# Two query chunks of layer 1 computed from the un-normalised residual, and the adaLN weights placed behind the query weights in the ring

## The chip, the cores and the metric

The kernel runs on one core of one Trainium2 chip. The metric is the device time of one execution in microseconds (us), the median of several runs. A core has five engines that run side by side and meet at semaphores: PE (TensorE, matrix products into the PSUM banks), ACT (ScalarE), DVE (VectorE), POOL (GpSimd) and SP (SyncE, which here only issues DMA transfers from HBM). All tiles live in SBUF, 128 partitions wide.

## The reference, cut to what matters

Two post-norm layers over 512 latent and 256 context tokens, width 1024. Layer 0 ends with a SwiGLU FFN and a layer norm; layer 1 begins with adaLN modulation of that result and one input projection:

```python
x = _layer_norm(ALPHA * x + ml[5] * _swiglu(_modulate(x, ml[3], ml[4]), ...), ln_g[l, 1], ln_b[l, 1])   # end of layer 0
# layer 1
ml = jnp.split(sc @ mod_w[l] + mod_b[l], 6, axis=-1)          # adaLN: six vectors of 1024, also for ctx
h_lat = x * (1.0 + ml[1]) + ml[0]
qk, v, og, g = jnp.split(h @ w_in, [o1, o2, o3], axis=-1)      # w_in: 1024 x (512 q + 512 k + 1024 v + 1024 og + 32 gates)
qk = jax.nn.silu(_centred_conv(qk, conv_w, conv_b))            # 3 taps over the tokens
g = (g.reshape(b, s, 4, H_M) + gate_b)                         # input and forget gates, then log_sigmoid and scans
```

Queries are needed for the latent tokens alone. With r the residual before the layer norm, x is (r - mean) * rstd * ln_g + ln_b, so a product with x can be made as a product with r and mended by mean and rstd of each token afterwards.

## The kernel before

Every product is made in three passes: weights and inputs are split into a high part (fp32r) and the rest, and PE forms high*high, high*low and low*high (`project`, line 692). Activations lie transposed: 8 chunks k of 128 features by 768 tokens (`xT`).

**The ring.** SP streams all weights through `ring`, 4 slots of 128x1024 fp32 (512 KB, a "unit"), in the fixed order of `STAGES`. `slot_free` makes SP wait until the unit four places ahead was used up. A projection unit is used up when POOL has made its low part (ACT copies the high part in `split_high`, POOL subtracts in `split_low`, line 2369, and counts `lo_made`). An adaLN unit (`mod` stages) is used by PE as it is, fp32, in `mod_rows_stacked` (line 644, 4 products of 256 columns, shown by the profile as 8 matmuls), which counts `unit_done`.

**Around the change.** The last third of the FFN of layer 0 writes its 8 output tiles m; after each, DVE updates `xT` (`z_update`), ACT squares it, DVE and POOL add up sum and sum of squares. Then PE does, in this order: adaLN units 0 to 2 of vector 2, the two cross-partition sums of the layer norm (`ln_sums`, line 964), the other 5 units of vector 2 and the 8 of vector 3. Beside it the layer norm runs through DVE and ACT, and chunk by chunk ACT makes the modulated input of layer 1 (`next_input`, lines 1294 and 1297) and DVE its low part (`low_chunk`, line 1767). ACT splits the first two projection units after its chunks 6 and 7. PE then starts the q/k chunks f = 0 and 1 (f = 0 to 3 are queries, 24 matmuls of 512 columns; 4 to 7 keys, 48 matmuls of 512 or 256) and the gate product on the padded tile `wg`, interleaved; then f = 2 to 7, and `token_major` (line 680) for the values.

**Gates and convolution.** ACT evacuates the gates (lines 1599), DVE and ACT form log-sigmoid (lines 2156, 1628, 1629, 2174), and DVE runs eight scans (line 2180, a cumulative sum and a running maximum, two directions, two token ranges). In between it does the 3-tap convolution of chunk f (`conv(f)`, lines 2169 to 2171) on what `conv_in(f)` of ACT put into `cpad`. `mod_columns` (PE transposes at line 652, DVE copy at line 1756, which counts `mod_ev`) turns a finished adaLN row into columns. The order on every engine is written out by hand.

## Time and profile before

| what | us |
|---|---|
| median of 3 runs | 1905.59 |
| lowest, highest | 1902.66, 1906.91 |
| the profiled execution, its own time | 1901.86 |
| span of its trace | 1900.1 |
| PE busy | 1776.1 (93%) |
| DVE, ACT, POOL busy | 688.1, 607.5, 716.1 |
| granted PE clock, mean | 0.97 |

The trace counts from the first instruction of the span. PE is busy for 93% of it, and the row of 40 slices shows one clear hole in it outside the first slice and the mLSTM: slice 25 (about 1140 to 1188 us), where its digit is 6, the granted clock falls to 0.7, and the DMA digit rises to 6. That is the stretch that the change touches.

### The profile page before, as it was taken

What the parts mean: (1) busy time and instruction counts of PE and PEld (TensorE: products, weight loads), DVE (VectorE), ACT (ScalarE), POOL (GpSimd) and SP (SyncE); (2) the same over time, 40 slices, a digit from 0 to 9 for tenths busy, and PEclk for the clock granted to TensorE, in tenths of its full rate; (3) what the DMA queues carried; (4) which work ended last, traced back from release to release, by engine and by line L of the source; (5) the groups of instructions that cost most, each with busy time, mean ns of one, the idle gap of its engine ahead of it and who ended that gap; (6) DMA issues with size and microseconds to landing.
All of it is one profiled execution on the core that took longest, in us unless ns stands there. A gap on an engine that the chain in (4) does not pass through costs nothing.

```text
span 1900.1 us, 24466 instructions
## 1 busy us (share of the span) xinstructions
PE 1776.1 (93%) x9848; PEld 1424.3 (75%) x9848; DVE 688.1 (36%) x1187; ACT 607.5 (32%) x863; POOL 716.1 (38%) x378
## 2 busy tenths in 40 slices
PE   4999999899899999999999996999776989999998
PEld 2788767455588888888888883787565878888886
DVE  2134254566467511111111036750178761111114
...
GB/s 295 121 47 62 58 122 89 103 165 177 111 56 65 58 67 78 56 67 57 76 58 53 50 61 207 56 69 66 55 1 23 89 70 108 111 89 100 88 83 72
DMA packets 210986, 163.36 MB, mean 86 GB/s; under 512 B 17742, under 2 KB 191022, under 8 KB 210902
## 3 DMA queue, kind: packets, MB, share of 16 engines
...
q14 instruction: 26, 0.21, 0.0%
...
## 4 chain that ended last, share of the span: by engine, by line
PE 82%; DVE 10%; ACT 4%; issue 2%; DMA 2%; POOL 1%; ACTq 0%; POOLq 0%; DVEq 0%
PE ps L692 58%; PE ps L680 3%; PE ps L682 3%; PE ps L681 3%; PE ps L851 2%; PE ps L878 2%; PE ps L903 1%; PE ps L888 1%; PE ps L805 1%; DMA ring<-in_mod_w 1%; PE ps L634 1%; PE ps L644 1%; DVE xT L2002 1%; PE ps L789 1%; DVE xT L1992 1%
## 5 line engine op out<-in xcount | busy, mean ns | idle before, releaser
L2375 POOL TENSOR_TENSOR wsplit<-ring,wsplit 128x1024 fp32r<-128x1024 f32 (+1 forms) x136 | 326.0, 2411 | 521.2 <-ACT wsplit L1470 521.0
L692 PE MATMUL ps<-hhi,wsplit 128*128 128x512 f32 (+1 forms) x1920 | 473.1, 354 | 6.4 <-DVE hu L2041 6.4
L692 PEld LDWEIGHTS ps<-hhi,wsplit 128*128 128x128 f32 x1920 | 314.9, 188 | 60.0 <-DVE hu L2041 6.9
L692 PE MATMUL ps<-hlo,wsplit 128*128 128x512 f32 x960 | 288.0, 354 | 0.0
L692 PE MATMUL ps<-uhi,wsplit 128*128 128x512 f32 x1008 | 250.4, 353 | 0.0
L2118 DVE TENSOR_TENSOR hu<-sg,ps 128x768 f32<-128x768 f32 (+1 forms) x40 | 32.9, 821 | 438.1 <-ACT sg L1539 438.1
L1470 ACT ACTIVATE wsplit<-ring 128x1024 fp32r<-128x1024 f32 (+1 forms) x136 | 135.1, 1023 | 173.5 <-PE ps L692 173.5
L692 PEld LDWEIGHTS ps<-uhi,wsplit 128*128 128x128 f32 x1008 | 164.9, 188 | 27.6
L692 PEld LDWEIGHTS ps<-hlo,wsplit 128*128 128x128 f32 x960 | 157.5, 188 | 26.5
L1965 DVE SCALAR_TENSOR_TENSOR xT<-ps,modc,xT 128x512 f32<-128x512 f32 x96 | 60.6, 659 | 272.1 <-PE ps L692 250.4
L692 PE MATMUL ps<-ulo,wsplit 128*128 128x512 f32 x504 | 150.8, 353 | 0.0
L2433 POOL TENSOR_SCALAR lnbuf<-lnbuf,den 128x768 f32<-128x768 f32 (+1 forms) x48 | 85.1, 1778 | 173.1 <-DVE den L1923 172.5
L1539 ACT ACTIVATE sg<-ps 128x768 f32<-128x768 f32 (+1 forms) x40 | 28.3, 706 | 377.2 <-PE ps L692 377.2
L692 PE MATMUL ps<-hx,wsp_in 128*128 128x256 f32 (+3 forms) x672 | 125.2, 347 | 6.5 <-POOL wsp_in L2369 6.5
L692 PEld LDWEIGHTS ps<-hx,wsp_in 128*128 128x128 f32 (+1 forms) x672 | 104.2, 189 | 26.8 <-POOL wsp_in L2369 6.9
L2369 POOL TENSOR_TENSOR wsp_in<-ring,wsp_in 128x1024 fp32r<-128x1024 f32 x22 | 53.2, 2416 | 168.3 <-ACT wsp_in L1285 168.3
L2369 POOL TENSOR_TENSOR wlo<-ring,whi 128x1024 fp32r<-128x1024 f32 x24 | 59.4, 2473 | 127.8 <-ACT whi L1285 127.8
L692 PEld LDWEIGHTS ps<-ulo,wsplit 128*128 128x128 f32 x504 | 82.5, 188 | 13.9
L692 PE MATMUL ps<-hx,wsp_out 128*128 128x512 f32 (+1 forms) x384 | 68.1, 340 | 2.5 <-DVE hx L2056 2.5
L692 PEld LDWEIGHTS ps<-hx,wsp_out 128*128 128x128 f32 x384 | 58.9, 188 | 11.7 <-DVE hx L2056 2.7
L2369 POOL TENSOR_TENSOR wsp_out<-ring,wsp_out 128x1024 fp32r<-128x1024 f32 x16 | 41.4, 2590 | 62.6 <-ACT wsp_out L1285 62.6
L680 PE MATMUL ps<-whi,hT 128*128 128x512 f32 x160 | 63.8, 399 | 0.8 <-ACT mv L1658 0.8
...
## 6 DMA issues: line engine op xcount, KB each, us to landing
...
```

The source lines that it names most:

```text
L680: pe.matmul(dst, s_hi, m_hi, start=first, stop=False)
L681: pe.matmul(dst, s_hi, m_lo, start=False, stop=False)
L682: return pe.matmul(dst, s_lo, m_hi, start=False, stop=last)
L692: mm = pe.matmul(dst[:, a:b], w, h[:, a:b], start=st, stop=sp_)
L851: mm = pe.matmul(pair[:, a:b], w, cqkv[:, k0 + k, a:b], start=(k == 0), stop=(k == nk - 1))
L878: mm = pe.matmul(PS[it % 2][:, a:b], qs_[0:DQ, q, tq], ks_[0:DQ, k, a:b], start=st, stop=sp_)
L1470: act.activation(w_part(s, 0)[:, 0:width], ring[:, (NB[f"ffn{l}"] + s) % RING, 0:width], ACT.Copy).then_inc(hi_made, 1)
L1965: ins = dve.scalar_tensor_tensor(xT[:, m, a:b], pair[:, a:b], modc[:, l, g, m, v:v + 1], xT[:, m, a:b], ALU.mult, ALU.add)
L2118: dve.tensor_tensor(hu[:, jj, 0:nt], sg[:, jj, 0:nt], PS[2 * jj][:, 0:nt], ALU.mult).then_inc(h_done, 1)
L2369: pool.tensor_tensor(w_lo[:, i % 2, :], ring[:, n % RING, :], w_hi[:, i % 2, :].bitcast(F32), ALU.subtract).then_inc(lo_made, 1)
L2375: pool.tensor_tensor(w_part(s, 1)[:, 0:width], ring[:, (NB[f"ffn{l}"] + s) % RING, 0:width], w_part(s, 0)[:, 0:width].bitcast(F32), ALU.su ...
L2433: pool.tensor_scalar(probs(i)[:, a:T], probs(i)[:, a:T], den[:, 1, i:i + 1], None, ALU.mult).then_inc(att_p, 1)
```

## The change

Chunks f = 0 and 1 are now made from the residual. While the last FFN tiles run, ACT makes `zqhi` = the high part of `xT` times the gain of layer 1 (`gain[:, 1, 0]`), DVE its rest `zqlo`, and two extra columns (minus the gain, and the shift) are put beside the 512 tokens, so that their products give what the mean and the shift have to be multiplied by. The weights of f = 0 and 1 pass the ring behind the FFN units and are split like those into `wsplit`. After the FFN, PE does f = 0 (48 matmuls of 256 or 258 columns), `ln_sums`, and f = 1; `late_query` on DVE mends them with mean and rstd, and ACT adds the shift in `conv_in`.

The adaLN units go elsewhere: units 0 to 2 of vector 2 are loaded into a tile of their own, `mod_pre`; units 3 and 4 and the weights of f = 2 and 3 share the ring; units 5 to 7 of vector 2 and all 8 of vector 3 come behind them. PE does f = 2 and 3 along with the arriving input chunks, then these 11 adaLN units, then the gate product, and then f = 4 to 7. ACT splits the two weight units after its input chunks 0 and 1. `mod_columns` of vector 3 is now called at f = 5 and done by DVE behind `conv(3)`, and its end is waited for at f = 6.

The core of the diff:

```diff
+    QW = LAT + 2
+    zqhi, zqlo, mod_pre = under(("zqhi", [P, KD, QW], F32R), ("zqlo", [P, KD, QW], F32R), ("mod_pre", [P, 3, UNIT], F32))
...
+    N_Q = 2
...
-              ("mod11", KD), ("mod05", KD), ("mod14", KD), ("mod15", KD), ("out0", N_OUT), ("ffn0", N_FFN), ("mod12", KD), ("mod13", KD), ("in1", N_IN1),
+              ("mod11", KD), ("mod05", KD), ("mod14", KD), ("mod15", KD), ("out0", N_OUT), ("ffn0", N_FFN + N_Q), ("mod12", 2), ("in1", 2), ("mod12b", 3), ("mod13", KD), ("in1b", N_IN1 - 4),
...
+    def q_bank(f):
+        return PS[(2, 3, 0, 1, 2, 0, 1, 2)[f]]
...
-        mod_units(1, 2)
-        mod_units(1, 3)
+        sp.wait_ge(ffn_tile, FT[0] + N_FFN - KD + TILE_CREDIT)
+        for k in range(MOD_PRE):
+            sp.dma_start(mod_pre[:, k, :], mod_w[1, k * P:(k + 1) * P, 2 * D:3 * D]).then_inc(mod_pre_in, 16)
         w_in = m_w_in[0].rearrange("(k p) n -> p k n", p=P)
-        for i in range(N_IN1):
-            n = NB["in1"] + i
+        for i in range(N_Q):
+            n = NB["ffn0"] + N_FFN + i
+            slot_free(n)
+            unit(n, view(n % RING, KD), w_in[:, :, i * P:(i + 1) * P])
+        mod_units(1, 2, MOD_PRE, MOD_PRE + 2)
+        for i in range(N_Q, N_IN1):
+            if i == 4:
+                mod_units(1, 2, MOD_PRE + 2, KD, "b")
+                mod_units(1, 3)
...
+        pe.wait_ge(zq_cols, 1)
         pe.wait_ge(z_ev, ZB[1] - 1)
-        mod_rows_stacked(1, 2, half(4), 0, 3)
-        ln_sums(1)
-        mod_rows_stacked(1, 2, half(4), 3, KD)
-        mod_rows_stacked(1, 3, half(5))
+        for f in range(N_Q):
+            pe.wait_ge(lo_made, FB[0] + N_FFN + f + 1)
+            if f == 1:
+                pe.wait_ge(z_ev, ZB[1])
+            for k in range(KD):
+                if f == 0:
+                    pe.wait_ge(zq_lo, k + 1)
+                for w, z, st, sp_ in ((0, zqhi, k == 0, False), (0, zqlo, False, False), (1, zqhi, False, k == KD - 1)):
+                    for a, b, at in LATE_MM[1]:
+                        mm = pe.matmul(q_bank(f)[:, at:at + b - a], w_part(f, w)[:, k * P:(k + 1) * P], z[:, k, a:b], start=st, stop=sp_)
+            mm.then_inc(ffn_tile, 1)
+            if f == 0:
+                ln_sums(1)
+        rows2, rows3 = PS[0][:, T:], PS[1][:, T:]
+        pe.wait_ge(ln_mean, 2)
+        pe.wait_ge(ln_var, 2)
+        pe.wait_ge(mod_pre_in, 16 * MOD_PRE)
+        for k in range(MOD_PRE):
+            for b in range(4):
+                pe.matmul(rows2[32 * b:32 * b + 2, :], s_kv[:, k, :], mod_pre[:, k, 256 * b:256 * (b + 1)], start=(k == 0), stop=False)
+        mod_rows_stacked(1, 2, rows2, MOD_PRE, MOD_PRE + 2)
...
-        for k in range(KD + 2 * LAG):
+        for k in range(KD + LAG):
             if k < KD:
                 pe.wait_ge(input_lo, 2 * KD + k + 1)
-            for f, kf in ((0, k), (1, k - LAG)):
+            for f, kf in ((2, k), (3, k - LAG)):
...
-            kf = k - 2 * LAG
-            if 0 <= kf < KD:
-                if kf == 0:
-                    pe.wait_ge(gate_lo, 1)
-                mm = project(PS[3], wg[:, 0, kf, :], wg[:, 1, kf, :], hT1[:, kf, :], hlo1[:, kf, :], kf == 0, kf == KD - 1, ALL_SEGS)
-                if kf == KD - 1:
-                    mm.then_inc(gate_mm, 1)
-        mod_columns(1, 2, half(4))
-        for f in range(2, 8):
-            if f == 2:
+        mod_rows_stacked(1, 2, rows2, MOD_PRE + 2, KD, "b")
+        mod_rows_stacked(1, 3, rows3)
+        pe.wait_ge(gate_lo, 1)
+        pe.wait_ge(late_q, 2)
+        for k in range(KD):
+            mm = project(PS[3], wg[:, 0, k, :], wg[:, 1, k, :], hT1[:, k, :], hlo1[:, k, :], k == 0, k == KD - 1, ALL_SEGS)
+        mm.then_inc(gate_mm, 1)
+        mod_columns(1, 2, rows2)
+        for f in range(4, 8):
+            if f == 5:
+                mod_columns(1, 3, rows3)
                 pe.wait_ge(mod_ev, MOD_AT[1, 2])
-            if f == 5:
+            if f == 6:
                 pe.wait_ge(mod_ev, MOD_AT[1, 3])
-            if f >= 3:
+            if f >= 5:
                 pe.wait_ge(f_ev, f - 2)
-            if f == 3:
-                mod_columns(1, 3, half(5))
             split_unit("in1", f)
             for k in range(KD):
                 mm = m_chunk(f, k)
             mm.then_inc(unit_done, 1)
         in1_parts = ((whi1, wlo1), hT1, hlo1)
-        token_major("in1", 8, [(t, t) for t in (4, 5, 0, 1, 2, 3)], *in1_parts, lambda b: pe.wait_ge(f_ev, (7, 8, 6)[b // 2]))
+        token_major("in1", 8, [(t, t) for t in range(TT)], *in1_parts, lambda b: pe.wait_ge(f_ev, (6, 7, 8)[b // 2]))
...
-            split_after = {0: (0, 1), 2: (6, 7)}.get(i)
+            split_after = (0, 1) if i in (0, 2) else None
...
+                if i == 2 and k == 0:
+                    act.wait_ge(ffn_tile, FT[0] + N_FFN + N_Q + TILE_CREDIT)
...
+                    if third == 2 and l == 0:
+                        if m == 0:
+                            act.wait_ge(gains_ok, 2)
+                        act.activation(zqhi[:, m, 0:LAT], xT[:, m, 0:LAT], ACT.Copy, scale=gain[:, 1, 0, m, 0:1]).then_inc(zq_hi, 1)
...
-        from_norm(1, hT1, hlo1_raw, lambda i: split_high("in1", i, whi1))
+        from_norm(1, hT1, hlo1_raw, lambda i: split_high("in1", i + N_Q, whi1))
...
-        split_high("in1", 2, whi1)
-        act.wait_ge(gate_mm, 1)
-        for g, dst in enumerate((li, gt, li, gt)):
-            act.activation(dst[0:H_M, g // 2, :], PS[3][32 * g:32 * g + H_M, 0:T], ACT.Identity,
-                           bias=gb[32 * g:32 * g + H_M, :]).then_inc(gate_ev, 1)
...
-            if f >= 2:
+            if f >= 4:
                 split_high("in1", f + 2, whi1)
-            act.wait_ge(unit_done, UB["in1"] + f + 1)
-            if f < 2:
+            if f < N_Q:
                 act.wait_ge(pad_ok, 4)
-            else:
-                act.wait_ge(conv_done, f - 1)
-            ins = act.activation(cpad[:, f % 2, 1:1 + LAT], PS[f % 3][:, 0:LAT], ACT.Copy)
+                act.wait_ge(late_q, f + 1)
+                act.activation(cpad[:, f, 1:1 + LAT], cacc[:, f, 0:LAT], ACT.Identity, bias=qc[:, f, 1:2]).then_inc(f_ev, 1)
+                return
+            act.wait_ge(unit_done, UB[part_of("in1", f)] + f + 1)
+            act.wait_ge(conv_done, f - 1)
+            ins = act.activation(cpad[:, f % 2, 1:1 + LAT], q_bank(f)[:, 0:LAT], ACT.Copy)
...
-        conv_in(0)
-        split_high("in1", 3, whi1)
+        for f in range(N_Q):
+            conv_in(f)
+            split_high("in1", f + 4, whi1)
+        act.wait_ge(gate_mm, 1)
+        for g, dst in enumerate((li, gt, li, gt)):
+            act.activation(dst[0:H_M, g // 2, :], PS[3][32 * g:32 * g + H_M, 0:T], ACT.Identity,
+                           bias=gb[32 * g:32 * g + H_M, :]).then_inc(gate_ev, 1)
...
+        def late_query(f):
+            dve.wait_ge(ffn_tile, FT[0] + N_FFN + f + 1 + TILE_CREDIT)
+            step(dve.tensor_copy(qc[:, f, :], q_bank(f)[:, LATE_COL[1]:LATE_COL[1] + 2]))
+            for a, b, at, _ in LATE_TOKENS[1]:
+                ins = dve.scalar_tensor_tensor(cacc[:, f, a:b], lnm[:, a:b], qc[:, f, 0:1], q_bank(f)[:, at:at + b - a], ALU.mult, ALU.add)
+            step(ins)
+            dve.tensor_tensor(cacc[:, f, 0:LAT], cacc[:, f, 0:LAT], lnr[:, 0:LAT], ALU.mult).then_inc(late_q, 1)
...
+                zq_low(KD - 1)
                 layer_norm(1, (hT1, hlo1, hlo1_raw))
...
-                mod_rows_stacked(1, 2, half(4))
-                mod_columns(1, 2, half(4))
-                mod_rows_stacked(1, 3, half(5))
+                for f in range(N_Q):
+                    late_query(f)
+                mod_rows_stacked(1, 2, PS[0][:, T:], "b")
...
         conv(0)
-        mod_columns(1, 3, half(5))
+        conv(1)
+        mod_columns(1, 2, PS[0][:, T:])
+        mod_rows_stacked(1, 3, PS[1][:, T:])
+        dve.wait_ge(gate_ev, 4)
+        dve.scalar_tensor_tensor(g_, z_, -1.0, z_, ALU.mult, ALU.min).then_inc(ls_in, 1)
+        dve.wait_ge(ls_ln, 1)
+        step(dve.scalar_tensor_tensor(b_, z_, 0.0, b_, ALU.min, ALU.subtract))
         for d in range(2):
             scan(gbc, lf, d, ALU.add, 0.0)
-        conv(1)
+        conv(2)
         step(dve.tensor_tensor(li[0:H_M, :, :], li[0:H_M, :, :], g_, ALU.subtract))
         for d in range(2):
             scan(gt, li, d, ALU.max, 0.0)
-        conv(2)
+        conv(3)
+        mod_columns(1, 3, PS[1][:, T:])
         dve.tensor_scalar(negm[0:H_M, :, :], gt[0:H_M, :, 0:LAT], -1.0, None, ALU.mult).then_inc(rows_ok, 1)
         dve.tensor_tensor(gbc[0:H_M, :, 0:LAT], gbc[0:H_M, :, 0:LAT], gt[0:H_M, :, 0:LAT], ALU.add).then_inc(floor_in, 1)
-        for f in range(3, 8):
+        for f in range(4, 8):
...
-        split_low("in1", 0, whi1, wlo1)
-        split_low("in1", 1, whi1, wlo1)
```

SP's DMA issues from the end of the FFN of layer 0 on, in the kernel before (`in_mod_w` are adaLN weights, `in_m_w_in` the projection weights of layer 1; a count is for issues alike):

```order
L496 DMA ring<-in_mod_w 128x1024 [waits lo_made] x4
L496 DMA ring<-in_mod_w 128x1024 [waits unit_done] x12
L496 DMA ring<-in_m_w_in 128x8x128 [waits unit_done] x4
L496 DMA ring<-in_m_w_in 128x8x128 [waits lo_made] x4
L496 DMA ring<-in_m_w_in 128x2x512 [waits lo_made] x8
```

The same place in the changed kernel:

```order
L607 DMA mod_pre<-in_mod_w 128x1024 [waits ffn_tile]
L607 DMA mod_pre<-in_mod_w 128x1024 x2
L517 DMA ring<-in_m_w_in 128x8x128 [waits lo_made] x2
L517 DMA ring<-in_mod_w 128x1024 [waits lo_made] x2
L517 DMA ring<-in_m_w_in 128x8x128 [waits lo_made] x2
L517 DMA ring<-in_mod_w 128x1024 [waits unit_done] x2
L517 DMA ring<-in_mod_w 128x1024 [waits lo_made] x2
L517 DMA ring<-in_mod_w 128x1024 [waits unit_done] x7
L517 DMA ring<-in_m_w_in 128x8x128 [waits unit_done] x4
```

The two first query units moved ahead of all adaLN units of the ring, two more stand between them, and a run of 7 adaLN units that each wait for PE (`unit_done`) stands ahead of the other projection weights.

PE between the last adaLN units and the input projection, before (lines 644 adaLN, 692 projection):

```order
L644 MATMUL ps<-ring,scol 2x256 x3
L644 MATMUL ps<-ring,scol 2x256 [waits landed0]
L644 MATMUL ps<-ring,scol 2x256 x3
L644 MATMUL ps<-ring,scol 2x256 [waits landed1]
L644 MATMUL ps<-ring,scol 2x256 x3
L692 MATMUL ps<-hT,whi 128x512 [waits input_lo,lo_made,z_ev,ln_rstd]
L692 MATMUL ps<-hlo,whi 128x512
L692 MATMUL ps<-hT,wlo 128x512
L692 MATMUL ps<-hT,whi 128x512 [waits input_lo]
```

The changed kernel, behind chunks f = 2 and 3 (lines 674 adaLN, 722 projection):

```order
L674 MATMUL ps<-ring,scol 2x256 x3
L674 MATMUL ps<-ring,scol 2x256 [waits landed1]
L674 MATMUL ps<-ring,scol 2x256 x3
L674 MATMUL ps<-ring,scol 2x256 [waits landed2]
L674 MATMUL ps<-ring,scol 2x256 x3
L722 MATMUL ps<-hT,wg 128x512 [waits late_q,gate_lo]
L722 MATMUL ps<-hT,wg 128x256
L722 MATMUL ps<-hlo,wg 128x512
L722 MATMUL ps<-hlo,wg 128x256
```

What follows the last adaLN unit is now the gate product, which was interleaved with f = 0 and 1.

DVE around the column copy of vector 3 (`modc`), before; `gbc` scans are cumulative sums, `cacc` rows are one convolution:

```order
L2174 SCALAR_TENSOR_TENSOR lf<-gt,lf 8x1536 [waits ls_ln]
L2169 TENSOR_SCALAR cacc<-cpad,vcol 128x512 [waits f_ev,dve_step]
L2170 SCALAR_TENSOR_TENSOR cacc<-cpad,vcol,cacc 128x512 [waits dve_step]
L2171 SCALAR_TENSOR_TENSOR cacc<-cpad,vcol,cacc 128x512 [waits dve_step]
L1756 TENSOR_TENSOR modc<-ps,modb 128x8 [waits mod_T]
L1756 TENSOR_TENSOR modc<-ps,modb 128x8
L2180 SCALAR_TENSOR_TENSOR gbc<-lf 8x256
L2180 SCALAR_TENSOR_TENSOR gbc<-lf,gbc 8x512 [waits dve_step]
```

The changed kernel; `gt` scans are the running maxima:

```order
L2254 SCALAR_TENSOR_TENSOR gt<-li 8x256 [waits dve_step]
L2254 SCALAR_TENSOR_TENSOR gt<-li,gt 8x512 [waits dve_step]
L2254 SCALAR_TENSOR_TENSOR gt<-li 8x256 [waits dve_step]
L2254 SCALAR_TENSOR_TENSOR gt<-li,gt 8x512 [waits dve_step]
L2246 TENSOR_SCALAR cacc<-cpad,vcol 128x512 [waits silu_ev,f_ev,dve_step]
L2247 SCALAR_TENSOR_TENSOR cacc<-cpad,vcol,cacc 128x512 [waits dve_step]
L2248 SCALAR_TENSOR_TENSOR cacc<-cpad,vcol,cacc 128x512 [waits dve_step]
L1809 TENSOR_TENSOR modc<-ps,modb 128x8 [waits mod_T]
L1809 TENSOR_TENSOR modc<-ps,modb 128x8
L2274 TENSOR_SCALAR lnbuf<-gt 8x1024
L2275 TENSOR_TENSOR gbc<-gbc,gt 8x2x512
```

The copy moved from behind the first convolution to behind all eight scans and the convolution of f = 3.

## Rows read from the trace of the kernel before

**Rows 1.** Chain that ended last, 1050 to 1260: start us, us, engine, tile, line.

```profile
1168.47 0.84 ACT hT L1297
1169.32 0.96 ACT whi L1285
1170.34 2.37 POOL wlo L2369
1172.84 21.60 PE ps L692 x96
...
1235.02 8.65 PE ps L692 x48
```

**Rows 2.** Stretches: length, busy PE PEld DVE ACT POOL, PEclk, DMA share, GB/s.

```profile
1150.00:1160.00 10.00, 3.72 (x32) 0.44 (x32) 10.00 (x11) 7.76 (x11) 2.93 (x2) 0.65 0.97 318
```

**Rows 3.** Timeline of PE, 1139 to 1180: start us, us, what, [idle before].

```profile
1141.73 1.48 PE L644 MATMUL ps<-ring,scol 128*2 128x256 f32 x24
...
1145.85 1.56 PE L964 MATMUL ps<-lnbuf,kc 128*128 128x512 f32 x4 [0.21 <-POOL lnbuf L2399]
...
1160.53 1.04 PE L644 MATMUL ps<-ring,scol 128*2 128x256 f32 x8 [1.72 <-DMA ring<-in_mod_w]
...
1165.72 1.03 PE L644 MATMUL ps<-ring,scol 128*2 128x256 f32 x8 [0.24 <-DMA ring<-in_mod_w]
1172.84 0.76 PE L692 MATMUL ps<-hT,whi 128*128 128x512 f32 x1 [6.09 <-POOL wlo L2369]
...
1177.09 0.39 PE L692 MATMUL ps<-hlo,whi 128*128 128x512 f32 x1
...
1179.86 0.40 PE L692 MATMUL ps<-hlo,whi 128*128 128x512 f32 x1
```

**Rows 4.** Stretch of layer 1 in products of 256 columns: length, PE busy, PEclk, DMA.

```profile
1525.00:1530.00 5.00, 5.00 (x44) 1.00 0.35 100
```

**Rows 5.** Timeline of ACT, 1095 to 1250.

```profile
1154.70 1.31 ACT L1294 ACTIVATE hlo_raw<-xT,gain 128x512 f32<-128x512 f32 x2 [2.15 <-DVE xT L2002]
...
1169.22 1.04 ACT L1285 ACTIVATE whi<-ring 128x1024 fp32r<-128x1024 f32 x1
...
1197.22 0.90 ACT L1599 ACTIVATE gt<-ps,gb 8x768 f32<-8x768 f32 x1
...
1202.73 1.58 ACT L1629 ACTIVATE lf<-lf,onec 8x1536 f32<-8x1536 f32 x1
```

**Rows 6.** Timeline of DVE, 1095 to 1270.

```profile
1172.37 1.15 DVE L1767 TENSOR_TENSOR hlo<-hlo_raw,hT 128x768 fp32r<-128x768 f32 x1 [2.06 <-ACT hT L1297]
...
1204.34 1.75 DVE L2174 SCALAR_TENSOR_TENSOR lf<-gt,lf 8x1536 f32<-8x1536 f32 x1 [4.44 <-ACT lf L1629]
1206.12 2.55 DVE L2169 TENSOR_SCALAR cacc<-cpad,vcol 128x512 f32<-128x512 f32 x1
...
1209.89 0.75 DVE L2171 SCALAR_TENSOR_TENSOR cacc<-cpad,vcol,cacc 128x512 f32<-128x512 f32 x1
...
1213.55 1.27 DVE L2180 TENSOR_TENSOR_SCAN gbc<-lf,gbc 8x512 f32<-8x512 f32 x1
...
1221.73 3.44 DVE L2180 TENSOR_TENSOR_SCAN gt<-li,gt 8x512 f32<-8x512 f32 x1
...
1227.62 0.49 DVE L2169 TENSOR_SCALAR cacc<-cpad,vcol 128x512 f32<-128x512 f32 x1
...
1228.93 0.75 DVE L2171 SCALAR_TENSOR_TENSOR cacc<-cpad,vcol,cacc 128x512 f32<-128x512 f32 x1
```

**Rows 7.** Timeline of POOL, 1085 to 1270.

```profile
1205.81 2.58 POOL L2369 TENSOR_TENSOR wlo<-ring,whi 128x1024 fp32r<-128x1024 f32 x1 [3.50 <-ACT whi L1285]
```

**Rows 8.** Tile ring, the issue by SP at 1142.4: an adaLN unit into an idle queue.

```profile
DMA to landing us min/median/max: 4.0/4.0/4.0
```

**Rows 9.** Groups by form, 1350 to 1800: count | busy us, mean ns | idle before.

```profile
L2016 DVE SCALAR_TENSOR_TENSOR zlo<-xT,gain,zhi 128x512 fp32r<-128x512 f32 x8 | 8.7, 1082 | 0.0
...
L1462 ACT ACTIVATE zhi<-xT,gain 128x512 fp32r<-128x512 f32 x8 | 5.7, 711 | 6.5 <-DVE xT L1965 6.5
```

86 lines of the change are left out of this document (53 added, 33 removed).

## The prediction

> **What bounds the kernel now.** I read the 40 slices first: PE is the engine that sets the time, with one hole at the layer boundary. The chain of waits of that stretch [rows 1] shows how the hole ends: ACT works through input chunks of 128 features, splits the first weight unit only behind its seventh chunk, POOL makes the low part (2.37 us), and PE starts the input projection at 1172.84. The timeline of PE [rows 3] shows it done with the FFN at 1141.7, so 31.1 us lie between, in which it did 16 adaLN units and the layer-norm sums. In that hole the granted clock was 0.65 and the DMA engines were busy for 0.97 [rows 2]: the adaLN units come as fast as HBM gives them, one per 1.3 us at the end ((1165.72 - 1160.53)/4, [rows 3]). From 1172.84 on PE is nearly gapless, and the last query/key chunk ends at 1235.02 + 8.65 = 1243.67 [rows 1], which is the mark that I carry the sum to. Everything behind it is the same work in the same order, so the difference at that mark is the difference of the kernel.
>
> **The change, step by step.** Times are those of the trace of before, so the sum is made against that execution.
>
> Tail of the FFN. Each output tile gets one more ACT pass and one more DVE pass; the alike operations of layer 1 take 711 and 1082 ns [rows 9]. ACT and DVE wait for PE there, so they cost nothing; if the last pair were late, PE would stand for at most their sum, 1.8 us, and its own 42 matmuls on the chunks before (4.8 us) cover that.
>
> A, the late query chunks. A layer-1 product of this shape runs 44 matmuls in 5.00 us [rows 4], so 48 take 5.45. f = 0 runs from 1141.7 to 1147.2, then come the two sums of 1.56 us each [rows 3], to 1150.3. Before they ended at 1145.85 + 1.56 = 1147.41. The layer norm starts 2.9 us later, and with it everything on ACT and DVE. f = 1 and the five first adaLN units run beside the layer norm, to about 1158.3.
>
> B, the input chunks. The first starts at 1154.70 + 2.9 = 1157.6 [rows 5]. Seven chunks took 1154.70 to 1169.31 [rows 5, 1], 2.09 each; eight, with two splits of 1.0 [rows 5] now among them, end at 1176.3, the last low part (1.15, [rows 6]) at 1177.5. PE follows chunk by chunk with f = 2 and 3, and has 12 matmuls left behind the last one. At full clock one takes 0.231 ((1179.86 - 1177.09)/12, [rows 3]), so they end at 1180.3. Here the change is well ahead: all four query chunks are done, while before f = 0 and 1 and the gate product ran until 1194.44 (1172.84 + 21.60, [rows 1]). At half clock PE would need (1177.09 - 1172.84)/10 = 0.425 for each of 48 from about 1163.4 on, and end at 1183.8; I take 1180.3, since dense work brought the clock back after 4 us in [rows 3].
>
> C, the adaLN stream. Four units are in the ring when PE gets to them, but the next slot comes free only when PE has used the first, at 1180.8. A transfer into an idle queue took 4.0 us [rows 8]: 1184.8. Six more follow. They come at 1.3 us at best; over the whole stream before, with 1.04 us of matmuls for each in the round, the pitch was up to 1.7, since other transfers stood between. I take 1.4, near the undisturbed end: 1193.2, and 1.0 us for the last unit's matmuls: 1194.2. That is 13.9 us in which PE works for some 6. Before, the same wait lay under the layer norm and was free. Bounds: 1193.1 and 1196.3.
>
> The Trainium skill ("DMA: Bandwidth & Descriptors", Specifications) gives a core about 358 GB/s from HBM. By that a unit of 524,288 bytes takes 1.46 us and the stream would end 0.4 us later than mine, an estimate from that page; the trace had one each 1.3.
>
> D, the gate product. It no longer shares PE's wait for input chunks; it starts behind the stream. It has the 48 matmuls of a key chunk: 8.65 us [rows 1]. After the hole before, the first ten matmuls took 4.25 instead of 2.31 [rows 3], so I add 1.9, PE having been idle for more than half of C: it ends at 1204.8. Before it ended at 1194.44. Lower bound without the 1.9.
>
> E, gates to log-sigmoid. The same operations: from 1194.44 to the end of the Ln at 1202.73 + 1.58 = 1204.31 [rows 5], 9.9 us: 1214.7. PE meanwhile does f = 4 (from 1205.5), waits for the evacuation of f = 2, which ACT now does behind the Ln (about 1215.3), and does f = 5, to 1224.0.
>
> F, the wait of f = 6. Its bank holds the row of vector 3 until DVE has copied the columns, and that copy stands behind everything on the gates. Before, DVE went from 1204.34 to 1228.93 + 0.75 = 1229.68, 25.3 us [rows 6], through the same eight scans with three convolutions; now there are two between, as two are done ahead of the gates. The one that goes took 1206.12 to 1210.64, 4.5 us, which leaves 20.8. In it one convolution and one scan were slow: a tensor_scalar of 2.55 where the same took 0.49, a scan of 3.44 where another took 1.27 [rows 6]. The slow tensor_scalar began 0.3 us behind the start of a POOL subtraction and ended 0.3 behind its end [rows 6, 7]. The weight splits of units 6 and 7 fall into this stretch; by my schedule unit 6 meets the convolution of f = 2 and unit 7 just misses the scan. So 20.8 - 2.2 = 18.6: the copy is made at 1233.3. Bounds: 16.2 with no meeting, 23.3 with every operation slow. PE stands from 1224.0 to 1233.3.
>
> G, f = 6 and 7. 8.65 each, and 1.9 again for the clock after 9 us of idling: 1252.5. Against 1243.67 that is +8.8.
>
> The copies, `mod_pre` and the waits that remain cost nothing: `mod_pre` is loaded while the FFN tail runs, `late_query` (two columns and three passes a chunk, done under C: at up to 1.1 us a pass [rows 9] some 6 of its 13.9 us), and the bank order of the values asks for each evacuation when it is due. Were that cover missing, the last evacuation would be late by about one convolution.
>
> **The sum.** 1901.86 + 8.8 = 1910.7 for an execution like the profiled one. The median of the runs is 3.7 above the profiled one, so I forecast 1905.6 + 8.8 = 1914.4, and write 1914. With all lower bounds (C -1.1, D -1.9, F -2.4, G -1.9) it is +1.5; with all upper ones (B +3.5, C +2.1, F +4.7) it is +19.1. The likeliest case's own range is 1909 to 1919.
>
> **The rivals.** Anything within 0.2% (3.8 us) is what a measurement here cannot tell from no change.
>
> *Faster, by a short wait at f = 6.* If DVE makes the column copy by the time f = 5 ends, F is not on the path: f = 6 and 7 follow at once, 1224.0 + 17.3 = 1241.3, 2.4 better than before; with C at its 1.3 pitch and no clock loss in D, E ends at 1211.7 and f = 7 at 1238.2, which is -5.4: 1900. For it: two whole query chunks leave the busy stretch, and convolutions 0 and 1 are made under C. Against it: it needs E's end to copy in about 9 us, and the eight scans and the two long passes over 1536 columns alone are more than that. It decides at a copy before about 1222.
>
> *No change to tell.* The lower bounds together: POOL misses DVE and the clock stays up. +1.5, so 1907. For it: [rows 6] shows each operation also at its short time. Against: the 6.09 us of idling before were followed by half clock [rows 3], and C and F are that long.
>
> *Slower still, by the shared port.* In F every POOL subtraction falls on DVE. Then F is 23.3 and the total +13.5: 1919. For it: in the gate stretch before, the convolution and the scan of [rows 6] were hit. The Trainium skill ("SBUF — State Buffer", Who interferes with whom) says that whichever of POOL and a DVE instruction of two SBUF inputs or of a two-port mode starts first keeps the other out until it has finished. By that rule the convolution's other passes block too. The trace agrees with the rule in the pair named in F; where the subtractions fall is not shown.
>
> **How the numbers follow.** Forecast 0.56, shared port 0.10, no change 0.20, faster 0.14. So slower by over 0.2%: 0.66, within: 0.20, faster: 0.14. The range of 1903 to 1920 leaves out most of the faster case and little above.
>
> **What would show it.** Right: the sums end near 1150, PE follows the input chunks from about 1163, a run of adaLN groups each idle for DMA from 1182 to 1194, the gate product ends at 1203 to 1206, and f = 6 has an idle time of some 9 us put down to the `modc` copy. Wrong, each by its own step: adaLN groups without idle before them (C), a half clock during f = 2 and 3 (B), or an f = 6 that follows f = 5 without a gap (F). The last alone turns the sign.

## The result and the profile after

The changed kernel takes 1917.44 us (median of 7 runs, 1914.02 to 1927.83) against 1905.59 of the kernel before in the same session. The ratio is 1.0077, with an interval of 1.0054 to 1.0100, so the change costs 14.7 us (10.3 to 19.1) of 1905.59. I had forecast slower by 8.8. The direction was right, the size too small. The profiled execution took 1917.19 us, its span 1915.5, at a granted clock of 0.963 (before 0.970).

The executions differ by up to 18 us before they reach the changed stage: the FFN of layer 0 ends at 1137 us in one of them and at 1156 in another. So every place below is counted from the end of that FFN's last matmul, at 1141.81 before and 1142.88 after (the expectations count from 0.17 us earlier in the changed kernel). By that count the tokens' product, which starts where f = 7 ends, moved from +101.7 to +114.6: 12.9 us. From there to the end of the span it takes 656.6 us before and 658.0 after.

These are PE's waits of the changed kernel from 1140 to 1290: tile and line, the releaser, us in total, times, longest.

```profile
PE ps L722 <- DVE modc L1809: 11.3, 1, 11.3
PE ps L722 <- POOL wlo L2450: 10.0, 1, 10.0
PE ps L674 <- DMA ring<-in_mod_w: 5.3, 7, 2.4
```

The first is the wait of f = 6 for the column copy, the second that of f = 2 for its weights' low part, the third the adaLN stream. Here is the stream on PE's timeline (start, us, what, idle before it), then the first step of f = 6.

```profile
1183.33 1.91 PE L674 MATMUL ps<-ring,scol 128*2 128x256 f32 x32
1187.65 0.61 PE L674 MATMUL ps<-ring,scol 128*2 128x256 f32 x8 [2.41 <-DMA ring<-in_mod_w]
...
1196.33 1.03 PE L674 MATMUL ps<-ring,scol 128*2 128x256 f32 x8 [0.66 <-DMA ring<-in_mod_w]
1197.29 1.01 PE L722 MATMUL ps<-hT,wg 128*128 128x512 f32 x2
...
1238.65 1.01 PE L722 MATMUL ps<-hT,whi 128*128 128x512 f32 x2 [11.33 <-DVE modc L1809]
```

Four units stand ready; the fifth comes 4.3 us behind the start, the last at 1196.33. Where [rows 3] has these groups beside the layer norm, PE now has nothing else to do. The windows show what HBM did in the meantime: stretch, length, busy PE, PEld, DVE, ACT, POOL, then PEclk, DMA share and GB/s. The first four lie between the end of the FFN and the end of f = 3, the fifth is the stream.

```profile
1142.90:1152.90 10.00, 10.00 (x72) 8.94 (x72) 5.24 (x6) 4.46 (x6) 3.71 (x3) 1.00 0.20 54
1152.90:1162.90 10.00, 6.28 (x74) 4.75 (x72) 10.00 (x10) 6.79 (x9) 5.23 (x10) 1.00 0.47 134
1162.90:1172.90 10.00, 3.71 (x9) 2.97 (x10) 9.47 (x8) 8.39 (x12) 9.23 (x2) 0.57 0.20 61
1172.90:1183.40 10.50, 10.50 (x45) 7.72 (x47) 9.28 (x19) 7.55 (x14) 0.00 (x0) 0.92 0.17 51
1183.40:1197.40 14.00, 8.70 (x89) 1.55 (x89) 4.40 (x9) 0.00 (x0) 0.00 (x0) 0.67 0.85 298
```

In [rows 2] the DMA share was 0.97 beside the layer norm. Now it is 0.17 to 0.47 for 40 us, with seven adaLN units (3.7 MB) still to come: the four slots of the ring hold weights whose turn has not come, and SP's queue stands behind them. SP's own wait for PE to use an adaLN unit shows it (total, times, longest), and the longest of these runs from 1143.9 to 1158.8:

```profile
SPq L517 <- PE ps L674: 35.5, 10, 14.9
```

The wait for POOL was not in my sum. POOL's timeline, then DVE's beside it:

```profile
1162.27 9.87 POOL L2450 TENSOR_TENSOR wlo<-ring,whi 128x1024 fp32r<-128x1024 f32 x2 [4.77 <-ACT whi L1331]
1199.80 2.42 POOL L2450 TENSOR_TENSOR wlo<-ring,whi 128x1024 fp32r<-128x1024 f32 x1 [27.67 <-ACT whi L1331]
```

```profile
1165.83 0.95 DVE L2055 TENSOR_TENSOR xT<-xT,lnbuf 128x768 f32<-128x768 f32 x1
1167.31 2.55 DVE L1820 TENSOR_TENSOR hlo<-hlo_raw,hT 128x768 fp32r<-128x768 f32 x1 [0.53 <-ACT hT L1345]
1169.78 3.17 DVE L2055 TENSOR_TENSOR xT<-xT,lnbuf 128x768 f32<-128x768 f32 x1
1172.87 0.95 DVE L1820 TENSOR_TENSOR hlo<-hlo_raw,hT 128x768 fp32r<-128x768 f32 x1
```

Two subtractions, 2.42 us each where POOL is alone, took 9.87. DVE ran operations of 0.95 us without a gap until it waited 0.53 us for ACT. From then on two of its operations take 2.55 and 3.17, and f = 2 starts at 1169.19.

The end of f = 3 hangs on something else that the same meeting did. These are ACT's sixth input chunk, DVE's last low part of an input chunk, and the first of PE's 12 matmuls that need it:

```profile
1172.98 1.31 ACT L1340 ACTIVATE hlo_raw<-xT,gain 128x512 f32<-128x512 f32 x2 [1.56 <-DVE xT L2055]
```

```profile
1179.35 0.96 DVE L1820 TENSOR_TENSOR hlo<-hlo_raw,hT 128x768 fp32r<-128x768 f32 x1 [1.11 <-ACT hT L1345]
```

```profile
1180.36 0.50 PE L722 MATMUL ps<-hT,whi 128*128 128x512 f32 x1
```

DVE's 3.17 us kept ACT waiting for 1.56, so the last low part was ready at +37.4, where I had +35.7. PE, late as it was, had just caught up with the chunks by then. Last the way from log-sigmoid to the column copy on DVE, to be held against [rows 6]:

```profile
1217.97 1.75 DVE L2265 SCALAR_TENSOR_TENSOR lf<-gt,lf 8x1536 f32<-8x1536 f32 x1 [4.44 <-ACT lf L1683]
...
1223.79 2.47 DVE L2246 TENSOR_SCALAR cacc<-cpad,vcol 128x512 f32<-128x512 f32 x1
...
1231.94 2.64 DVE L2254 TENSOR_TENSOR_SCAN gt<-li 8x256 f32<-8x256 f32 x1
1234.62 1.61 DVE L2254 TENSOR_TENSOR_SCAN gt<-li,gt 8x512 f32<-8x512 f32 x1
...
1238.35 0.24 DVE L1809 TENSOR_TENSOR modc<-ps,modb 128x8 f32<-128x8 f32 x2
```

It takes 20.6 us from 1217.97 to 1238.59. Two scans are slow here, 2.64 and 1.61 where their like took 0.68 and 1.27. POOL's subtraction for unit 7 (1230.83, 3.21 us) ran beside the first of them, and the short POOL operation that follows it (1234.03, 1.13 us) beside the second.

### The profile page after: what moved, and what is told of

It reads as the page before. It is cut to its first block, busy times and chain, and to the rows that moved or that the text cites. A ratio compares the mean times of both kernels' runs of the same rounds, so it can differ in the third digit from the quotient of the medians.

```text
span 1915.5 us, 24604 instructions
## 1 busy us (share of the span) xinstructions
PE 1782.3 (93%) x9896; PEld 1436.9 (75%) x9896; DVE 700.5 (37%) x1207; ACT 612.4 (32%) x871; POOL 722.9 (38%) x378
## 4 chain that ended last, share of the span: by engine, by line
PE 83%; DVE 10%; ACT 3%; DMA 2%; issue 2%; POOL 1%; ACTq 0%; POOLq 0%; DVEq 0%
PE ps L722 59%; PE ps L710 3%; PE ps L712 3%; PE ps L711 3%; PE ps L881 2%; PE ps L908 2%; PE ps L933 1%; PE ps L918 1%; PE ps L819 1%; DMA ring<-in_mod_w 1%; PE ps L674 1%; PE ps L835 1%; PE ps L664 1%; DVE xT L2055 1%; DVE xT L2045 1%
## 5 line engine op out<-in xcount | busy, mean ns | idle before, releaser
L2456 POOL TENSOR_TENSOR wsplit<-ring,wsplit 128x1024 fp32r<-128x1024 f32 (+1 forms) x138 | 333.4, 2429 | 522.6 <-ACT wsplit L1518 522.4
```

The source lines that it names most:

```text
L2456: pool.tensor_tensor(w_part(s, 1)[:, 0:width], ring[:, (NB[f"ffn{l}"] + s) % RING, 0:width], w_part(s, 0)[:, 0:width].bitcast(F32), ALU.su ...
```

## The experiments

All of them start from the changed kernel. Ratios are to the kernel before, run on the same chip beside each set; the interval is of 95%. This table has the places of each profile, in us from the end of the FFN.

| kernel | f = 2 starts | f = 3 ends | gate product ends | f = 6 starts | tokens' product starts | ratio |
|---|---|---|---|---|---|---|
| before | | | 52.6 | | 101.7 | 1 |
| after | 26.3 | 40.5 | 65.2 | 95.8 | 114.6 | 1.0077 (1.0054 to 1.0100) |
| columns early | 26.4 | 40.6 | 64.2 | | 100.4 | 1.0006 (0.9986 to 1.0026) |
| interleaved | 26.3 | 40.5 | 55.7 | 93.9 | 112.3 | 1.0057 (1.0035 to 1.0079) |
| low parts by DVE | 22.6 | 39.0 | 63.8 | 94.4 | 112.9 | 1.0051 (1.0027 to 1.0076) |
| combined | 26.3 | 40.5 | 55.6 | | 95.5 | 0.9963 (0.9942 to 0.9985) |
| late queries alone | 38.2 | 55.2 | 64.8 | 95.4 | 114.7 | 1.0083 (1.0052 to 1.0113) |
| no stream | 26.3 | 40.5 | 54.0 | 84.6 | 103.1 | 1.0016 (0.9994 to 1.0038) |
| convolutions early | 26.4 | 40.6 | 65.7 | 92.4 | 111.2 | 1.0062 (1.0035 to 1.0090) |
| combined, DVE low | 22.6 | 38.9 | 54.3 | | 95.6 | 0.9980 (0.9956 to 1.0004) |
| preload | 26.4 | 40.6 | 51.1 | 83.2 | 101.7 | 1.0010 (0.9983 to 1.0038) |
| preload combined | 26.3 | 40.5 | 51.0 | | 86.7 | 0.9938 (0.9914 to 0.9962) |
| the same, DVE low | 24.8 | 38.9 | 49.4 | | 85.1 | 0.9918 (0.9891 to 0.9945) |
| POOL held | 26.3 | 40.6 | 66.2 | 94.5 | 114.1 | 1.0089 (1.0060 to 1.0117) |

**Columns early.**

```diff
         step(dve.scalar_tensor_tensor(b_, z_, 0.0, b_, ALU.min, ALU.subtract))
+        mod_columns(1, 3, PS[1][:, T:])
...
         conv(3)
-        mod_columns(1, 3, PS[1][:, T:])
```

> One edit to the changed kernel: DVE copies the columns of vector 3 right behind the operation that makes the log forget gates, ahead of the eight scans and of convolutions 2 and 3, in place of behind them. My theory (the wait of f = 6 for this copy is on the path): in the changed kernel f = 6 waits 11.33 us for it, from 1227.3 to 1238.65. With the copy early, f = 6 follows f = 5 with less than 1.5 us between, the half clock behind that wait (10.24 us) goes or shrinks, and the tokens' product starts 11 to 13 us before the 1257.48 of the changed kernel, near 1245. The time is 11 to 14 us below the changed kernel's 1917.4, so within 3 us of the kernel before. Rival 1 (what stands behind the copy on DVE holds PE as well): f = 7 or the first values then wait for the evacuation of f = 4 or 5, since the copy's place changes and DVE's work does not; the gap reappears there with 5 us or more and the gain is under 6 us. Rival 2 (the 2.9 us later layer norm and the lower clock are the cause, the wait only follows): gain under 3 us.

The wait for the copy is gone, and the tokens' product starts 14.2 us earlier. PE's waits:

```profile
PE ps L722 <- POOL wlo L2450: 10.0, 1, 10.0
PE ps L674 <- DMA ring<-in_mod_w: 5.4, 7, 2.7
PE ps L710 <- ACT cpad L1661: 2.2, 1, 2.2
```

The last line is new: rival 1 exists, at 2.2 us in place of 5. The time falls by 0.0071 of 1905.59, 13.5 us: the place of one copy on DVE is nearly the whole loss.

**Interleaved.**

```diff
-        mod_rows_stacked(1, 3, rows3)
+        mod_rows_stacked(1, 3, rows3, 0, 1)
...
         for k in range(KD):
             mm = project(PS[3], wg[:, 0, k, :], wg[:, 1, k, :], hT1[:, k, :], hlo1[:, k, :], k == 0, k == KD - 1, ALL_SEGS)
...
+            if k >= 1:
+                mod_rows_stacked(1, 3, rows3, k, k + 1)
```

> One edit to the changed kernel: of the gate product's eight steps each now stands between two adaLN units of vector 3, in place of all eight behind the stream. My theory (stream and gate product stand one behind the other, 13.9 and 10.7 us, and PE idles in the first for 7 groups of 0.8 us): the product needs 1.1 to 1.3 us a step and a unit comes each 1.3, so both together take 14 to 17 us from 1183.3 and the gate product ends at 1197 to 1200 in place of 1208.05. Log-sigmoid, scans and the column copy come 8 to 11 us earlier, and so do f = 6 and f = 7: time 7 to 11 us below the changed kernel's 1917.4. f = 6 still waits for the copy, by about the same. Rival 1 (only the wait at f = 6 matters, PE's order ahead of it does not, since DVE and not PE sets the copy): then the gain is small, under 3 us, and the wait at f = 6 grows by what the front gained. Rival 2 (a ring slot comes free later, as each unit now waits for a gate step): the stream's pitch grows from 1.3 to over 1.8 us and the gain is halved.

The gate product ends 9.5 us earlier, as I had it, yet f = 6 starts only 1.9 earlier. My size was wrong, and rival 1 had it right, but for another reason than its own: the wait for the copy did not grow (11.4), f = 4 started late. ACT's timeline, then DVE's:

```profile
1205.20 1.06 ACT L1334 ACTIVATE whi<-ring 128x1024 fp32r<-128x1024 f32 x1 [16.89 <-DMA ring<-in_m_w_in]
1206.16 0.71 ACT L1658 ACTIVATE cpad<-cacc,again 128x512 f32<-128x512 f32 x1
```

```profile
1206.90 2.11 DVE L2249 TENSOR_SCALAR cacc<-cpad,vcol 128x512 f32<-128x512 f32 x1 [13.41 <-ACT cpad L1658]
...
1214.84 1.74 DVE L2266 SCALAR_TENSOR_TENSOR gbc<-gt 8x1536 f32<-8x1536 f32 x1
```

The gate product ends at 1203.50, but ACT stands until 1205.20 for weight unit 4, which comes behind the stream, with the evacuation for the second convolution queued behind that split; DVE has that convolution ahead of the gates. So from the end of the gate product to log-sigmoid it is 17.5 us in place of 9.9.

**Low parts by DVE.**

```diff
+                    if i == 1 and k in (2, 3):
+                        n = NB["in1"] + k
+                        dve.wait_ge(hi_made, SB["in1"] + k + 1)
+                        dve.tensor_tensor(wlo1[:, k % 2, :], ring[:, n % RING, :], whi1[:, k % 2, :].bitcast(F32),
+                                          ALU.subtract).then_inc(lo_made, 1)
...
```

> One edit to the changed kernel: DVE in place of POOL makes the low parts of weight units 2 and 3, between its chunks of the third and fourth layer-norm step. In the changed kernel the two subtractions on POOL took 9.87 us beside DVE's chunk operations (2.4 us each elsewhere) and PE waited 10.0 us for them, starting f = 2 at 1169.19 where I had 1163.4. My theory (POOL was kept waiting by DVE's operations with two inputs in memory): f = 2 starts at 1163 to 1165, the 2.55 and 3.17 us operations on DVE beside POOL's are gone, but the end of f = 3 hangs on the last input chunk, which DVE now makes some 2 us later for its own two subtractions: f = 3 ends between 1181 and 1184 in place of 1183.4, and the time is 0 to 3 us below the changed kernel. Rival (PE's late start is what put the end of f = 3 at 1183.4): the 5 us earlier start comes through, f = 3 ends at 1179 or before, and the time falls by 4 to 5 us.

DVE's timeline:

```profile
1161.15 1.22 DVE L2063 TENSOR_TENSOR wlo<-ring,whi 128x1024 fp32r<-128x1024 f32 x1
1162.28 0.95 DVE L2055 TENSOR_TENSOR xT<-xT,lnbuf 128x768 f32<-128x768 f32 x1
...
1164.02 1.21 DVE L2063 TENSOR_TENSOR wlo<-ring,whi 128x1024 fp32r<-128x1024 f32 x1
```

DVE needs 1.22 us for what took POOL 2.42 alone and 4.9 here, and none of its other operations is slow. f = 2 starts 3.7 us earlier, where I had 4.2 to 6.2. The last low part of an input chunk is ready at +35.8 in place of +37.4, f = 3 ends 1.5 earlier and the tokens' product starts 1.7 earlier: my size. The time (-0.0026) can't tell that from nothing.

**Combined.** The interleaving, all four query convolutions ahead of the gates and of the splits of units 4 and 5, and the columns early.

> Three edits to the changed kernel together: gate steps between the adaLN units of vector 3; all convolutions of the four query chunks ahead of the gates (under the stream); and the columns of vector 3 copied ahead of the scans. My theory: stream plus gate product 14 to 17 us in place of 24.6, no wait of f = 6 (11.3) and no half clock behind it (2), and the scans finish 4 us earlier. The tokens' product starts at 1232 to 1237 in place of 1257.48 in the changed kernel and 1243.5 before: time 20 to 24 us below the changed kernel's 1917.4 and 6 to 10 us below the kernel before, 1896 to 1900. If the gains don't add (DVE's evacuations hold PE once the copy no longer does): 1902 to 1906, with a new gap on PE of 4 us or more ahead of f = 7 or the values. If the theory is wrong and the clock alone decides: no more than 5 us below the changed kernel.

The tokens' product starts at +95.5, 19.1 us earlier than after (1.4 later than my range) and 6.2 earlier than before, and the ratio says 7.1 us (2.9 to 11.1) below the kernel before. The gains do add once the convolutions no longer stand between the stream and log-sigmoid. PE's only wait:

```profile
PE ps L722 <- POOL wlo L2454: 12.9, 2, 10.0
```

**Late queries alone.** The stages of the ring in the order `mod12`, `mod12b`, `mod13`, `in1`, `in1b`, and PE's adaLN groups back beside the layer norm.

> One half of the change alone: the two late query chunks stay, but all adaLN units go back ahead of the weights of query chunks 2 and 3 in the ring and are worked on beside the layer norm, as in the kernel before. My theory (the stream cost 13.9 us because it stands bare behind f = 3): it lies beside the layer norm again. Counted from the end of the FFN (which moves by some 15 us from one execution to the next): f = 2 starts later, as its weights land behind eleven more units of 1.3 us, by 5 to 9 us, f = 3 ends at +46 to +48 us (+40.7 in the changed kernel), the gate product at +55 to +57 (+65.4), f = 6 still waits for the column copy, about 10 us, and the tokens' product starts at +103 to +107 (+114.8 changed, +101.8 before). Time 8 to 12 us below the changed kernel. Rival 1 (the queue of the adaLN units costs the same wherever it stands, for PE now waits for the weights of f = 2 as it waited for the stream): f = 3 ends at +52 or later and the gain is under 4 us. Rival 2 (the wait at f = 6 takes back what the gate product gains): the wait grows to 14 us or more.

My theory failed here and rival 1 held. f = 3 ends at +55.2, 14.6 us later than after. PE's waits:

```profile
PE ps L721 <- DVE modc L1808: 11.4, 1, 11.4
PE ps L673 <- DMA ring<-in_mod_w: 7.6, 9, 2.8
PE ps L721 <- POOL wlo L2449: 4.7, 1, 4.7
```

The stream costs the same ahead of f = 2 as behind f = 3. Before, PE used adaLN units from the end of the FFN on ([rows 3], the group from 1141.7); now the late chunks and the sums keep it until +14. From +0.4, where POOL has split the weights of f = 1, no slot comes free until then, and the DMA share in the first two stretches of 10 us is 0.19 and 0.47 as in the changed kernel. It is the late chunks in front of a ring of four slots that cost the stream, wherever it is put.

**No stream.** The eight units of vector 3 are not loaded; its row is made from the three preloaded ones.

> The changed kernel with the eight adaLN units of vector 3 not loaded; PE makes its row from the three preloaded units in their place, so vector 3 of layer 1 comes from other weights and its 4 MB are not moved. It prices the stream. My theory: behind f = 3 only the three units of vector 2 are waited for, so from the end of f = 3 to the start of the gate product it takes 5 to 9 us in place of 13.9, and weight units 4 and 5 land 10 us earlier; the gate product ends 6 to 9 us earlier counted from the end of the FFN, the wait at f = 6 stays near 11, and the time falls by 6 to 9 us against the changed kernel. Rival (the DVE chain to the copy starts no earlier): the gate product comes earlier but the wait at f = 6 grows by as much, and the time falls by less than 3 us.

Gate product 11.2 us earlier, wait of f = 6 unchanged (11.4), tokens' product 11.5 earlier, time -0.0061 (11.6 us). It was more than the 6 to 9 that I gave it: behind f = 3 no wait at all is left, 4.8 us of matmuls.

**Convolutions early.**

```diff
-        for f in range(N_Q):
+        for f in range(4):
             conv_in(f)
-            split_high("in1", f + 4, whi1)
+            if f >= 2:
+                conv_out(f - 2)
+        split_high("in1", 4, whi1)
+        split_high("in1", 5, whi1)
...
```

> One edit to the changed kernel: convolutions 2 and 3 are made ahead of the gates (evacuations on ACT and convolutions on DVE under the adaLN stream, with the splits of units 4 and 5 behind them); the column copy stays behind the scans. My theory: the way from the log-sigmoid to the copy loses two convolutions, of 4.4 and 2.0 us in the changed kernel, and is 14 to 16 us in place of 20.6, so the wait of f = 6 falls from 11.3 to 5 to 7 us; stream and gate product stay at 13.9 and 10.7. The time falls 4 to 7 us against the changed kernel. Rival (what POOL's subtractions and DVE's scans take from each other): the subtractions of units 6 and 7 now fall on scans and on the pass over 1536 columns, which grow by 2 us each, and the gain is under 3 us.

3.4 us at the tokens' product. The way to the copy is 16.8 us; two convolutions left it, and both subtractions of POOL, with the short POOL operation behind each, now meet scans (DVE, to be held against 0.68 and 1.27):

```profile
1218.99 2.80 DVE L2257 TENSOR_TENSOR_SCAN gbc<-lf 8x256 f32<-8x256 f32 x1
1221.82 1.61 DVE L2257 TENSOR_TENSOR_SCAN gbc<-lf,gbc 8x512 f32<-8x512 f32 x1
...
1227.27 2.78 DVE L2257 TENSOR_TENSOR_SCAN gt<-li 8x256 f32<-8x256 f32 x1
```

The rival had the mechanism, and my lower bound for the gain was too high by 0.6.

**Combined, DVE low.** The combined kernel with the low parts by DVE.

> The three edits of the combined kernel (gate steps between the adaLN units, all query convolutions and the column copy early) and the low parts of units 2 and 3 by DVE. Alone the last edit brought f = 2 forward by 3.6 us and the end of f = 3 by only 1.7 us, counted from the end of the FFN (+38.97 for +40.69), as the last input chunk then sets that end. In the combined kernel nothing that waits behind hangs on DVE, so the 1.7 us come through: the tokens' product starts at +93 to +95 from the end of the FFN in place of +95.7, and the time is 1 to 3 us below the combined kernel's, a ratio of 0.995 to the kernel before. Rival (the units 4 and 5 that f = 4 waits for land by the stream, not by PE): the wait ahead of f = 4 grows from 3.4 to 5 us and nothing is gained, 0.996.

f = 3 ends 1.6 us earlier, the gate product 1.3 and f = 4 starts 1.2 earlier, yet the tokens' product is at +95.6 as in the combined kernel. The rival's longer wait did not come (2.9 us in both): f = 4 itself took 11.4 us for 10.1, with a granted clock of 0.74 in it for 0.85. Whether that is the edit or chance, one profile can't tell.

**Preload.** Seven units of vector 3 go to memory that the FFN frees, in place of the ring.

```diff
+    _, mod_pre3 = under(("mod_pre3_pad", [P, 2 * KD * T + 2 * KD * (T + 4) + 4 * UNIT], F32), ("mod_pre3", [P, KD - 1, UNIT], F32))
...
+        sp.wait_ge(ffn_tile, FT[0] + N_FFN - KD + 1 + TILE_CREDIT)
+        pre3(0, 3)
...
+                sp.wait_ge(ffn_tile, FT[0] + N_FFN + 1 + TILE_CREDIT)
+                pre3(3, 5)
+                sp.wait_ge(ffn_tile, FT[0] + N_FFN + 2 + TILE_CREDIT)
+                pre3(5, 7)
...
```

> One edit to the changed kernel: seven of the eight adaLN units of vector 3 don't go through the ring's four slots. They are loaded into memory that the end of the FFN gives free (three into the FFN's gate and hidden buffers, two each into its weight slots 2 and 3 when the late chunks are done with them), and PE works on them beside the layer norm. In the changed kernel the DMA engines were busy for 0.20, 0.47, 0.20 and 0.17 in the four stretches of 10 us from the end of the FFN to the end of f = 3, and for 0.85 under the stream. My theory (the stream stands behind f = 3 because the ring's slots are held, not because HBM has no time): the seven come in that idle time, four units stand in the ring when f = 3 ends, and PE needs 2 to 3 us for them in place of 13.9. From the end of the FFN: gate product ends at +52 to +54 (+65.4 changed), the tokens' product starts at +102 to +104 (+114.8), f = 6 still waits 10 to 12 us for the column copy. Time 10 to 13 us below the changed kernel, so within 3 us of the kernel before. Rival 1 (the wait for POOL grows, since transfers, adaLN work and the splits of units 2 and 3 meet): f = 2 starts 3 us later or more and takes back as much. Rival 2 (DVE sets the copy, the front does not): the wait at f = 6 grows by what the stream gave, gain under 4 us.

The same four stretches as above, from the end of the FFN to that of f = 3:

```profile
1137.20:1147.20 10.00, 10.00 (x72) 8.94 (x71) 5.21 (x6) 4.46 (x6) 3.66 (x3) 1.00 0.51 155
1147.20:1157.20 10.00, 6.30 (x74) 4.77 (x73) 10.00 (x10) 6.75 (x9) 5.23 (x10) 1.00 0.60 183
1157.20:1167.20 10.00, 6.22 (x68) 3.47 (x68) 9.47 (x7) 8.44 (x13) 9.27 (x2) 1.00 0.36 123
1167.20:1177.70 10.50, 9.61 (x38) 6.44 (x36) 9.27 (x19) 7.53 (x14) 0.00 (x0) 1.00 0.17 50
```

HBM had the time: the seven units come in it, f = 2 starts where it did, and the stream of 13.9 us is 1.8. The gate product ends 14.1 us earlier: 12.1 are the stream, and 2.1 are its own, as it takes 8.7 us at a granted clock of 1.00 for 10.8 at 0.79. The wait for the copy is 10.0, and the tokens' product starts 12.9 us earlier, where the kernel before has it. My theory held, with stream and gate product a little ahead of their ranges.

**Preload combined, and the same with the low parts by DVE.** Both add to the preload the convolutions and the columns ahead of the scans; the second adds the low parts by DVE.

> The preload of the run above, and with it the query convolutions ahead of the gates and the column copy ahead of the scans; the gate product in one piece. My theory says that the three costs add up and now all are gone but POOL's 10 us at f = 2: from the end of the FFN f = 3 ends at +40.7, the gate product at +51.5 to +54, f = 4 to 7 follow with less than 4 us of waits, and the tokens' product starts at +88 to +92 (+95.7 in the combined kernel, +101.8 before). Time 10 to 14 us below the kernel before, ratio 0.993 to 0.995. If DVE becomes the bound (evacuations and convolutions behind the scans): a new wait of 4 us or more ahead of f = 7 or the tokens' product, which then starts at +94 to +97, and the ratio is 0.996 as that of the combined kernel.

> As the run above, with the low parts of units 2 and 3 made by DVE between its layer-norm operations. In the changed kernel alone this brought the end of f = 3 from +40.7 to +39.0 us after the end of the FFN; in the combined kernel it gave nothing (+95.62 for +95.53 at the tokens' product), as f = 4 then waited that much longer for units 4 and 5, which landed behind the stream. Without a stream these units land early, so my theory has the 1.7 us come through: 1 to 2 us below the run above. Rival (DVE's two subtractions push its own chunk work back, and the adaLN matmuls beside it change the clock): the same time as the run above or 1 us more.

They beat both kernels: +86.7 and +85.1, ratios 0.9938 and 0.9918, 11.8 us (7.2 to 16.4) and 15.6 us (10.5 to 20.8) below the kernel before. These are the waits of the first, with the small one of the tokens' product for evacuations on ACT that the early columns had shown:

```profile
PE ps L1113 <- DMA mod_pre<-in_mod_w: 3.6, 1, 3.6
PE ps L735 <- POOL wlo L2471: 2.9, 3, 1.7
PE ps L723 <- ACT cpad L1679: 2.5, 2, 1.5
```

The 1.6 us of the low parts come through here. The two ratios' intervals overlap, so that step rests on the profiles. None of the later edits was tried on the kernel before. Its waits show only 0.3 us for a column copy, so early columns have little to take away there. But how much of the lead is due to the late queries is not shown.

**POOL held.**

```diff
+            if i == 7:
+                pool.wait_ge(mod_ev, MOD_AT[1, 3])
             split_low("in1", i, whi1, wlo1)
```

> One edit to the changed kernel: POOL's subtraction for unit 7 waits until DVE has made the column copy of vector 3. In the changed kernel it ran for 3.21 us from 1230.83 on beside DVE's scans, of which two took 2.64 and 1.61 us where their like took 0.68 and 1.27; I had this subtraction just miss them, which is 2.0 us of the size by which my forecast was short. Unit 7 is needed only by f = 7, 8.65 us behind the start of f = 6. My theory (POOL and DVE take the time from each other): with the wait both scans take 0.68 and 1.27, the way from log-sigmoid to the copy is 18.1 to 18.6 us in place of 20.6, f = 6 waits 9 to 9.5 us in place of 11.3, the subtraction itself takes 2.4 to 3.2 us and f = 7 follows f = 6 at once; the tokens' product starts 2.0 to 2.3 us earlier. Rival (the slow scans come from something else, the clock or an address): they stay at 2.64 and 1.61, and nothing moves.

DVE's scans, as they run now:

```profile
1239.89 0.68 DVE L2254 TENSOR_TENSOR_SCAN gt<-li 8x256 f32<-8x256 f32 x1
1240.61 1.27 DVE L2254 TENSOR_TENSOR_SCAN gt<-li,gt 8x512 f32<-8x512 f32 x1
```

The way to the copy is 18.3 us (1225.91 to 1244.25) in place of 20.6, and the wait of f = 6 is 9.0 in place of 11.3. So the slow scans were POOL's. Little of it reached the tokens' product (0.5 us): in this execution the gate product ended 1.0 later and f = 6 and 7 took 0.8 longer. The ratio, 1.0089, does not differ from the changed kernel's. The mechanism is shown, the gain in time is not.

## Why the prediction was right and wrong

A, the late queries, held: the sums end at +8.3 for a forecast 8.5. C, the stream, took 13.9 us, the forecast to a tenth. There is some luck in that: the fifth unit came 4.3 us behind the start for a forecast 4.5, and the pitch was 1.45 for 1.4, and the two cancel. D, the gate product, took 10.8 for 10.6, E 9.9 for 9.9, and G, f = 6 and 7, 18.8 for 19.2. That the stream stands on the path is shown by the preload, which took 12.9 us out with one edit. That f = 6 waits for the copy is shown by the early columns (14.2).

B failed: f = 3 ended at +40.5 and I had 38.5. Two of its steps did not hold. "PE follows chunk by chunk" from about 1163.4 took low parts of the weights in 2.4 us for granted; they took 9.87 for two, and PE started 4.7 us late. PE then ran its first 12 matmuls at half clock, which was my sign of a wrong B. Yet that is not what moved the end: the preload kernel has a granted clock of 1.00 there and ends f = 3 at +40.6. The step that cost the time is "Seven chunks took ... 2.09 each; eight, with two splits ... end at 1176.3". The first chunk came 0.4 us late, the chunks then took 1.5 more, for DVE, slowed by POOL, held ACT for 1.56, and the rest is in the last 12 matmuls. With POOL's two subtractions on DVE that wait is gone, the last low part comes at +35.8, and f = 3 ends at +39.0.

I had weighed the shared port in F alone, where [rows 6] shows it. Before, ACT split unit 0 behind its seventh chunk, when DVE already waited for ACT ([rows 5, 6]); the change brings the splits forward into DVE's unbroken run. The rule that I cited from the Trainium skill ("SBUF — State Buffer", Who interferes with whom) bears on that place too. It says there that the order of issue decides who blocks. The trace agrees only in part: the two do slow each other, but POOL's subtraction is recorded from 1162.27 on, and the five operations that DVE started after that still took 0.95 us each. The slow ones came after DVE's pause of 0.53 us; that POOL got in by that pause is my reading, and no run tests it.

F was too small: 20.6 us for 18.6. The failing step is "unit 7 just misses the scan". Its subtraction hit one scan and the short POOL operation behind it a second, and with both held back F took 18.3, so the forecast was right for the meeting that I assumed. The rival of the shared port had the mechanism; its 23.3 was every operation slow, and this is one meeting more.

B and F are 4.0 us together; with them the forecast's +110.7 at the tokens' product becomes 114.7, and 114.6 was measured. Of what is left to the 14.7 of the ratio, 1.4 lies behind the tokens' product in the profiled pair (658.0 for 656.6), which other executions show from 654.9 to 660.1 without an order that I can read; it stays open and is inside the interval.

The rival of the faster outcome needed a copy before 1222, and it came at 1238.6. But it named the right lever: with the columns early, two late query chunks off the busy stretch cost nothing any more, though they bring nothing either. With the preload and the early convolutions beside them the kernel is ahead; that the late chunks have a part in this is not shown.
